# Unread products of constants in TensorE's waits, the overflow branch moved into the middle of the experts, and the wait of the up-projection split

## The chip, the core and the metric

The kernel runs on one core of one Trainium2 chip. A core has five engines that run their own instruction streams and meet at semaphores: TensorE (PE in the profile, its weight loads PEld), VectorE (DVE), ScalarE (ACT), GpSimd (POOL) and SyncE (SP), which issues the DMAs. The metric is the device time of one execution in microseconds, lower is better.

## The reference, cut to what matters

Two blocks of two layers each, over 256 tokens of width 1024, all in float32. What the change touches:

```python
def first_block(...):
    for l in range(DEPTH):                      # DEPTH = 2
        h = modulate(rms_norm(x, norm1_g[l]), sh1, sc1)
        x = x + g1[:, None, :] * token_mixer(h, ...)
        h = modulate(rms_norm(x, norm2_g[l]), sh2, sc2)
        x = x + g2[:, None, :] * hier_moe(h, ...)   # router, then 32 experts, top 2 of 8 in one of 4 groups

def hier_moe(...):
    ...
    sizes = jnp.bincount(flat_e, length=N_EXPERTS)  # any size is allowed
    hu = lax.ragged_dot(xs, w1, sizes)              # 1024 x 1024 for each expert
    ys = lax.ragged_dot(jax.nn.silu(h_gate) * h_up, w2, sizes)   # 512 x 1024

def second_block(...):
    for i in range(DEPTH):
        h = modulate_2(rms_norm_2(x, norm_g[i, 0]), sh1, sc1)
        y = attention_mixers(...) if i % 2 == 0 else fourier_mix(h) @ w_f
        x = x + g1 * rms_norm_2(y, norm_g[i, 1])
        h = modulate_2(rms_norm_2(x, norm_g[i, 2]), sh2, sc2)
        x = x + g2 * rms_norm_2(conv_ffn(h, ...), norm_g[i, 3])
```

## The kernel before

The tokens stay in SBUF, features on the partitions (`xT`, 8 tiles of 128x256). Each engine has a hand-written program (`pe_program`, `act_program`, ...); nothing is scheduled by a tool, so the order in the code is the order on the engine. An engine waits with `wait_ge` on counts that others raise.

**Banks.** PSUM banks `ps0` to `ps3` are handed out round robin by `bank.turn(name)`: who takes a turn waits until the bank's earlier holder is through, which `bank.until(name, counter, step)` has declared.

**A norm** (`NormMod`, with `Rstd`) runs over all engines: ACT squares the eight tiles of x (L729), PE sums them with 128x1 products (`pe_stats`, "stats" below), ACT takes the root (L777), DVE the reciprocal and two diagonal matrices (L782, L785), PE multiplies ones by the diagonal (`pe_spread`), DVE and ACT scale and shift, tile by tile, and for the split matmuls ACT and DVE make a high and a low part of each tile (L827, L860). Then the projection's products begin. **A post-norm** (`PostNorm`) comes after an output projection: ACT squares and sums the result in PSUM (L2621), ACT and DVE copy it out scaled (ACT L2633, DVE L2662), PE transposes it back (L2648) and DVE adds it to `xT` (L2665). In `postA` the result stands in all four of `ps0` to `ps3`; its own transposes go to other banks (`hbank`), and each bank of the four is free once its part is "copied". In `postF` the result stands in `ps4` to `ps7`.

**The router** ends in a chain of small operations on DVE (L1839 to L1883) that finds each token's two experts (`sel`) and their places, during which PE has only the counting products (128x32) to do. **The experts** go in 16 pairs. A pair `p` on PE: `pe_up` (32 matmuls, two row groups at a time), `pe_scatter(p - 1)`, `pe_gather(p + 1)`, a transposition (`pe_turn`), `pe_down` (16 matmuls). The weights, 12 MB a pair, come through 13 slots that SP refills in `sp_moe` as PE frees them. `pe_gather(p + 1)` needs one-hot places that DVE makes after it has worked off `pe_up(p)` (L2002, L2004, then L1952). A pair holds up to 64 tokens of an expert. Where an expert has more, a branch (`flag > 0`, code in `pe_over_all` and its like on ACT, DVE and SP) does the rest; with these inputs it is jumped over. It stands at the end of the 16 pairs, after the last scatter:

```python
pe_scatter(pe, l, m, NE // 2 - 1)
pe.wait_ge(*dve_moe["flag", l])
flag = pe.op.value_load(ints[0:1, l * 16 + 15:l * 16 + 16], min_val=0, max_val=8)
with pe.op.If(flag > 0):
    pe_over_all(pe.part(), l, m)
```

What follows in layer 0 is `norm1[1]`; in layer 1 it is `pe_heads`, whose first products work on the context and need no norm.

Of the kernel before, what the change touches and what calls it, by code (L numbers as in the profile page):

```python
# [18 lines left out]
NE = 32  # L19
# [205 lines left out]
def build(nc, A, out):  # L225
    CST_W = sum(w for _, w in CONST_COLS.values())
    with ExitStack() as ctx:
# [184 lines left out]
        def mm3(pe, out_, a, b, start, stop, **kw):  # L412
            mm(pe, out_, a[0], b[1], start, False, **kw)
            mm(pe, out_, a[1], b[0], False, False, **kw)
            return mm(pe, out_, a[0], b[0], False, stop, **kw)

        def sp_fm(sp, name, W, a0, by):

            load(sp, name, by_rows(W[:, a0:a0 + 256]), 8, 256)
            for m in range(2):  # L420
                unit((*name, m), name, 8, 256, lambda v, m=m: v[:, :, m * 128:(m + 1) * 128], by)
# [373 lines left out]
        class NormMod:  # L795
# [32 lines left out]

            def pe(self, pe, gap=0):
                self.r.pe_stats(pe)  # L830
                self.r.pe_spread(pe)
                pe_mods(pe, gap)

            def dve(self, dve, gap=0):
# [853 lines left out]
        def sp_moe(sp, l):  # L1688
# [6 lines left out]
            n_load = 0  # L1695
            for p in range(NE // 2):
                for which, W, parts in (("w1", W1, 4), ("w2", W2, 2)):
                    for n in range(parts):
                        for e in (2 * p, 2 * p + 1):
                            if n_load == all_.index(12):  # L1700
                                sp.wait_ge(*pe_unit["o", l, 3, 1])
                            load(sp, (which, l, e, n), by_rows(W[e, n * 256:(n + 1) * 256, :]), 2, 1024, all_)
                            n_load += 1
# [3 lines left out]
            else:  # L1707
                sp_kv(sp, 0)
            sp.wait_ge(*dve_moe["flag", l])
            flag = sp.op.value_load(ints[0:1, l * 16 + 15:l * 16 + 16], min_val=0, max_val=8)  # L1710
            with sp.op.If(flag > 0):
                part = sp.part()
                for j in range(NOV):
                    part.wait_ge(*dve_over[l]["ints"])
                    part.wait_ge(*(pe_over[l]["scatter", j - 1] if j else pe_moe["scatter", l, 15]))
                    e = part.op.value_load(ints[0:1, l * 16 + j:l * 16 + j + 1], min_val=0, max_val=31)
# [81 lines left out]
        def pe_router(pe, l, m):  # L1798
            pe_tokens(pe, l, m, 3)
            pe_stats(pe, l, m, 3)  # L1800
            if l == 1:
                pe_turn_tokens(pe, ("ctx",), "ctx", act_pro)
# [171 lines left out]
        def pe_up(pe, l, m, p):  # L1974
            x3 = v3(m.x["x", l, p], 8)
            for half in range(2):
                pe.wait_ge(*bank.turn("up", l, p, half))
            pe.wait_ge(*act_moe["xg", l, p])
            pe.wait_ge(*dve_moe["xg", l, p])
            for k in range(8):  # L1980
                for half in range(2):
                    for e in range(2):
# [87 lines left out]
        def pe_moe_all(pe, l, m):  # L2070
            pe_gather(pe, l, m, 0)
            for p in range(NE // 2):
                pe_up(pe, l, m, p)
                if p:
                    pe_scatter(pe, l, m, p - 1)
# [8 lines left out]
            pe_scatter(pe, l, m, NE // 2 - 1)  # L2084
            pe.wait_ge(*dve_moe["flag", l])
            flag = pe.op.value_load(ints[0:1, l * 16 + 15:l * 16 + 16], min_val=0, max_val=8)
            with pe.op.If(flag > 0):
                pe_over_all(pe.part(), l, m)

        def act_moe_all(act, l, m):  # L2090
            act_gather(act, l, m, 0)
            for p in range(NE // 2):
                act_up(act, l, m, p)
                if (l, p) == (0, NE // 2 - 1):
# [8 lines left out]
                if (l, p) == (1, 2):  # L2103
                    normC.act_apply(act)
            act.wait_ge(*dve_moe["flag", l])
            flag = act.op.value_load(ints[0:1, l * 16 + 15:l * 16 + 16], min_val=0, max_val=8)
            with act.op.If(flag > 0):
                act_over_all(act.part(), l, m)

        def dve_moe_all(dve, l, m):  # L2110
            dve_gather(dve, l, m, 0)
            for p in range(NE // 2):
                dve_up(dve, l, m, p)
                if p + 1 < NE // 2:
# [3 lines left out]
                if (l, p) == (1, 1):  # L2118
                    normC.dve(dve)
            dve.wait_ge(*dve_moe["flag", l])  # L2120
            flag = dve.op.value_load(ints[0:1, l * 16 + 15:l * 16 + 16], min_val=0, max_val=8)
            with dve.op.If(flag > 0):
                dve_over_all(dve.part(), l, m)
            g2 = mods[:, l * 48 + 40:l * 48 + 48]
# [9 lines left out]
        def dve_over_all(dve, l, m):  # L2134
            P3, G3, xv, gv, tv, hv, yv = over_bufs(m)
            D_ = dve_over[l]
            ind3, gt3, prod3, p13 = v3(m.ind, NOV), v3(m.gate, 2), v3(m.prod, 2), v3(m.p1, 2)
            dve.wait_ge(*pe_moe["scatter", l, NE // 2 - 1])
            for j in range(NOV):
# [63 lines left out]
        def pe_over_all(pe, l, m):  # L2203
            P3, G3, xv, gv, tv, hv, yv = over_bufs(m)
            x3, h3 = v3(xv[:, 0:512], 8), v3(hv[:, 0:256], 4)
            slot = [v3(slot_at[2 + n][0], 2) for n in range(6)]
            for j in range(NOV):
                pe.wait_ge(*dve_over[l]["P", j])
# [399 lines left out]
        class PostNorm:  # L2608
# [31 lines left out]

            def pe(self, pe):
                for k in range(8):
                    for j in range(2):
# [308 lines left out]
        def pe_program(pe):  # L2952
# [4 lines left out]
            for l in range(2):  # L2957
                if l == 1:
                    norm1[l].pe(pe, 3)
                pe_mixer(pe, l, mix[l], norm1[l])  # L2960
# [4 lines left out]
            for l in range(2):  # L2965
                if l == 1:
                    normA[1].pe(pe)
                    pe_fourier(pe, normA[1])
# [3 lines left out]
                postA[l].pe(pe)  # L2972
                normF[l].pe(pe)
                pe_ffn_all(pe, l, ffn)
# [146 lines left out]
```

## Time and profile before

| | |
|---|---|
| median of 3 runs | 2311.27 us (2306.36 to 2318.2) |
| the profiled execution | 2302.7 us, of which 2300.9 us from its first to its last instruction |
| PE busy | 2134.7 us, 93% |
| DVE, ACT, POOL busy | 42%, 30%, 12% |
| granted TensorE clock, mean | 0.972 of 2.4 GHz |

The granted clock has two levels, 1.00 (2.4 GHz) and 0.50 (1.2 GHz). A window's row that says 0.50 lay wholly at the lower one.

### The profile page before, as it was taken

The numbers are of one execution on the slowest core, as the hardware profiler recorded it, in microseconds if no ns is written. First come the engines' busy times: TensorE is split into PE (matmuls) and PEld (weight loads), VectorE is DVE, ScalarE is ACT, GpSimd is POOL, SyncE is SP. The second block draws the span as 40 slices with busy tenths as digits, with TensorE's granted clock in tenths as the row PEclk, the third lists the DMA queues.
The fourth block names the chain that finished last, engine by engine and source line by source line (L and its number), as shares of the span: only waits on it lengthen the run. The fifth ranks groups of instructions, "written<-read, shape, count | busy, mean of one in ns | idle before, by whom it ended". The sixth has DMA issues, their size and how long they took to land.

```text
span 2300.9 us, 30193 instructions
## 1 busy us (share of the span) xinstructions
PE 2134.7 (93%) x12867; PEld 1500.7 (65%) x12867; DVE 963.1 (42%) x1892; ACT 685.9 (30%) x1224; POOL 284.1 (12%) x145
## 2 busy tenths in 40 slices
PE   6999888999999989998899999999998899998998
PEld 4787674555544567777645555554774699978997
DVE  2466632212111136566312221221245577756776
ACT  3434421101101034353211110110203555555554
POOL 4554420000000034554000000000000000000000
PEclk8999989999999989999899999999999999998999
DMA  9965669999999976657689999999355375334651
GB/s 347 325 226 206 242 241 380 409 409 409 409 409 409 408 275 224 220 220 293 271 347 389 409 409 409 409 409 404 126 206 213 130 235 187 109 115 167 199 173 48
DMA packets 242742, 657.30 MB, mean 286 GB/s; under 512 B 12923, under 2 KB 116837, under 8 KB 230184
## 3 DMA queue, kind: packets, MB, share of 16 engines
q1 hardware_dynamic: 239936, 651.74, 74.8%
q8 instruction: 105, 1.72, 0.3%
q0 software_dynamic: 1184, 2.08, 0.3%
q10 hardware_dynamic: 1480, 1.45, 0.2%
q14 instruction: 37, 0.30, 0.0%
HBM read 654.17 MB, written 1.06 MB: 285 GB/s over the span
## 4 chain that ended last, share of the span: by engine, by line
PE 86%; DVE 10%; ACT 3%; issue 1%; DMA 0%; POOL 0%; ACTq 0%; DVEq 0%
PE ps L410 85%; DVE AR L1971 2%; DVE AR L747 1%; DVE AR L2018 1%; PE ps L2648 0%; DVE ARr L1646 0%; DVE AR L1231 0%; ACT AR L818 0%; ACT AR L2621 0%; ACT HBr L387 0%; PE ps L2472 0%; DMA hT<-in_onehot 0%; DVE ringr L393 0%; DVE AR L1114 0%; ACT hTr L827 0%
## 5 line engine op out<-in xcount | busy, mean ns | idle before, releaser
L410 PE MATMUL ps<-ring,AR 128*64 128x512 f32 (+2 forms) x2016 | 514.7, 577 | 31.4 <-DVE AR L2018 31.4
L410 PE MATMUL ps<-XLr,HBr 128*128 128x256 f32 x1280 | 375.5, 293 | 22.1 <-DVE ringr L393 6.9
L410 PE MATMUL ps<-AR 128*128 128x128 f32 (+6 forms) x2088 | 380.9, 345 | 14.0 <-DVE AR L1952 7.5
L410 PEld LDWEIGHTS ps<-ring,AR 128*64 128x64 f32 (+1 forms) x2016 | 196.8, 140 | 268.9 <-issue 264.0
L410 PEld LDWEIGHTS ps<-AR 128*128 128x128 f32 (+2 forms) x2088 | 290.0, 192 | 119.5 <-issue 76.4
L410 PE MATMUL ps<-hTr,ringr 128*128 128x256 f32 x1280 | 366.5, 286 | 0.0
L410 PE MATMUL ps<-hTr,HBr 128*128 128x256 f32 x1280 | 366.2, 286 | 0.0
L393 POOL TENSOR_TENSOR ringr<-ring,HBr 128x1024 fp32r<-128x1024 f32 x110 | 266.3, 2436 | 777.6 <-ACT HBr L387 777.4
L387 ACT ACTIVATE HBr<-ring 128x1024 fp32r<-128x1024 f32 x260 | 266.3, 1050 | 196.6 <-PE ps L410 179.9
L410 PEld LDWEIGHTS ps<-XLr,HBr 128*128 128x128 f32 x1280 | 249.4, 195 | 43.6 <-issue 24.8
L410 PEld LDWEIGHTS ps<-hTr,ringr 128*128 128x128 f32 x1280 | 250.2, 195 | 2.1 <-issue 1.0
L410 PEld LDWEIGHTS ps<-hTr,HBr 128*128 128x128 f32 x1280 | 249.8, 195 | 0.0
L393 DVE TENSOR_TENSOR ringr<-ring,HBr 128x1024 fp32r<-128x1024 f32 x150 | 179.5, 1223 | 82.0 <-ACT HBr L387 81.7
L2002 DVE SCALAR_TENSOR_TENSOR AR<-AR,ps 128x512 f32<-128x512 f32 x32 | 22.0, 688 | 438.1 <-ACT AR L1997 438.1
L410 PE MATMUL ps<-HB,AR 128*64 128x512 f32 x464 | 154.7, 597 | 8.0 <-DVE AR L2018 8.0
L1997 ACT ACTIVATE AR<-ps 128x512 f32<-128x512 f32 x32 | 19.1, 598 | 418.8 <-PE ps L410 418.8
L410 PE MATMUL ps<-HBr,ARr 128*128 128x512 f32 x416 | 135.9, 395 | 0.0
L2047 DVE COPY AR<-ps 128x512 f32<-128x512 f32 x32 | 22.1, 692 | 237.8 <-PE ps L410 237.8
L410 PE MATMUL ps<-XL,AR 128*64 128x512 f32 x240 | 108.1, 593 | 6.1 <-DVE AR L2018 3.2
L410 PE MATMUL ps<-hT,AR 128*64 128x512 f32 x240 | 108.1, 593 | 3.2 <-DVE AR L2018 3.2
L410 PE MATMUL ps<-ring,crep 128*32 128x512 f32 x704 | 97.2, 632 | 13.5 <-DVE mods L709 12.9
L2042 ACT ACTIVATE AR<-ps 128x512 f32<-128x512 f32 x32 | 19.1, 597 | 282.9 <-PE ps L410 282.9
(311 smaller groups left out, 2593.9 us busy)
## 6 DMA issues: line engine op xcount, KB each, us to landing
ring<-in_w_expert_in SPq DMA_DIRECT2D x155, 1024.0 KB, 14.8
ring<-in_w_expert_out SPq DMA_DIRECT2D x81, 1024.0 KB, 11.0
ring<-in_mod_w SPq DMA_DIRECT2D x48, 1024.0 KB, 6.6
ring<-in_ffn_w_up SPq DMA_DIRECT2D x44, 1024.0 KB, 5.2
ring<-in_w_in SPq DMA_DIRECT2D x40, 1024.0 KB, 5.6
ring<-in_w_ada SPq DMA_DIRECT2D x40, 1024.0 KB, 8.2
HB<-in_w_expert_in SPq DMA_DIRECT2D x35, 1024.0 KB, 14.6
HB<-in_w_expert_out SPq DMA_DIRECT2D x23, 1024.0 KB, 12.3
```

Of the source, the lines that this page charges most:

```text
L387: act.op.activation(hi, raw, ACT.Copy).then_inc(*act_hi.inc(*name))
L393: lane.op.tensor_tensor(lo, sel(chunk(of, k, w)), hi.bitcast(F32), ALU.subtract).then_inc(*count.inc(*name))
L410: return pe.op.matmul(out_, lhsT, rhs, start=start, stop=stop, **kw)
L747: dve.op.reciprocal(rs[:, 0:n], rs[:, 0:n]).then_inc(*dve_norm.inc(tag, "rstd"))
L1971: dve.op.tensor_scalar(m.x["x", l, p][:, k * 128:(k + 1) * 128], bank["xg", l, p, 1][:, c], m.coef[:, k:k + 1], m.shift[:, k:k + 1], ALU.m ...
L1997: act.op.activation(m.th["th", l, p], bank["up", l, p, 0][:, :], ACT.Tanh, scale=0.5).then_inc(*act_moe.inc("th", l, p))
L2002: dve.op.scalar_tensor_tensor(t, t, 1.0, bank["up", l, p, 0][:, :], ALU.add, ALU.mult).then_inc(*dve_moe.inc("gated", l, p))
L2018: dve.op.tensor_copy(m.h["h", l, p], bank["turn", l, p][:, :]).then_inc(*dve_moe.inc("turn", l, p))
L2042: act.op.activation(m.y["y", l, p][:, 0:512], bank["down", l, p, 0][:, :], ACT.Copy).then_inc(*act_moe.inc("y", l, p))
L2047: dve.op.tensor_copy(m.y["y", l, p][:, 512:1024], bank["down", l, p, 1][:, :]).then_inc(*dve_moe.inc("y", l, p))
```

## The change

Four things, all on the order and the waits; the values that reach the output are those of before.

1. `pe_busy(pe, n, name)` issues `n` products of constants (ones by 512 columns of the constant table, full array, float32) into a bank that nobody reads. It is called: 5 and 3 times in the routers of layers 0 and 1 (between the stats and the counting products), 2 before the stats of `norm1[1]` and 1 between its stats and its spread, 1 and 2 likewise around the spread of `normA[1]`, 1 and 3 around that of both `normF`, 3 at the head of each of the four post-norms. In all 34 products.
2. The overflow branch goes from the end of the 16 pairs to the head of pair 9, on all four engines; `pe_scatter(8)` moves ahead of it.
3. SP takes its branch before it loads pair 9, not after all loads.
4. `pe_up` waits for ACT's half of the gathered tokens before the first four k, and for DVE's half only before k = 4.

```diff
+        def pe_busy(pe, n, *name):
+            pe.wait_ge(*q_cst0["all"])
+            pe.wait_ge(*bank.turn("busy", *name))
+            for _ in range(n):
+                t = mm(pe, bank[("busy", *name)][:, :], C("ones"), cst[:, 0:512], True, True)
+            t.then_inc(*pe_pro.inc("busy", *name))
+            bank.until(("busy", *name), pe_pro, "busy", *name)
...
-            def pe(self, pe, gap=0):
+            def pe(self, pe, gap=0, busy=0):
                 self.r.pe_stats(pe)
+                if busy:
+                    pe_busy(pe, 1, self.tag, "diagonal")
                 self.r.pe_spread(pe)
                 pe_mods(pe, gap)
+                if busy > 1:
+                    pe_busy(pe, busy, self.tag, "applied")
...
             for p in range(NE // 2):
+                if p == OVER_AT:
+                    sp_over(sp, l, W1, W2)
...
             pe_stats(pe, l, m, 3)
+            pe_busy(pe, 5 - 2 * l, "router", l)
...
-            pe.wait_ge(*act_moe["xg", l, p])
-            pe.wait_ge(*dve_moe["xg", l, p])
             for k in range(8):
+                pe.wait_ge(*(act_moe if k < 4 else dve_moe)["xg", l, p])
...
         def pe_moe_all(pe, l, m):
             pe_gather(pe, l, m, 0)
             for p in range(NE // 2):
+                if p == OVER_AT:                       # OVER_AT = 9
+                    pe_scatter(pe, l, m, p - 1)
+                    pe.wait_ge(*dve_moe["flag", l])
+                    flag = pe.op.value_load(ints[0:1, l * 16 + 15:l * 16 + 16], min_val=0, max_val=8)
+                    with pe.op.If(flag > 0):
+                        pe_over_all(pe.part(), l, m)
                 pe_up(pe, l, m, p)
-                if p:
+                if p and p != OVER_AT:
                     pe_scatter(pe, l, m, p - 1)
...
             pe_scatter(pe, l, m, NE // 2 - 1)
-            pe.wait_ge(*dve_moe["flag", l])
-            flag = pe.op.value_load(ints[0:1, l * 16 + 15:l * 16 + 16], min_val=0, max_val=8)
-            with pe.op.If(flag > 0):
-                pe_over_all(pe.part(), l, m)
...
             def pe(self, pe):
+                pe_busy(pe, 3, self.tag)
                 for k in range(8):
...
                 if l == 1:
-                    norm1[l].pe(pe, 3)
+                    pe_busy(pe, 2, "norm1", l)
+                    norm1[l].pe(pe, 3, 1)
...
-                    normA[1].pe(pe)
+                    normA[1].pe(pe, 0, 2)
...
-                normF[l].pe(pe)
+                normF[l].pe(pe, 0, 3)
```

PE in layer 0, from the last products of `pe_down(8)` to the head of pair 9, before the change (`64x512` are expert products, `128x256` the scatter, `128x128` with AR alone the gather):

```order
L410 MATMUL ps<-ring,AR 64x512
L410 MATMUL ps<-HB,AR 64x512
L410 MATMUL ps<-AR 128x256 [waits dve_moe,act_moe]
L410 MATMUL ps<-AR 128x256 x7
L410 MATMUL ps<-AR 128x128 [waits dve_moe]
L410 MATMUL ps<-AR 128x128 x15
```

There the last products of `pe_up(9)` are followed by `pe_scatter(8)`, and that by `pe_gather(10)`. With the change the scatter stands at the head of pair 9, behind `pe_down(8)`, and the branch behind it (`128x64` is the first row of the part that is jumped over):

```order
L410 MATMUL ps<-ring,AR 64x512
L410 MATMUL ps<-AR 128x256 [waits dve_moe,act_moe]
L410 MATMUL ps<-AR 128x256 x7
L2096 TENSOR_LOAD ints
L2096 ISA x2
L2097 COMPARE_AND_BRANCH
L410 MATMUL ps<-AR 128x64 [waits dve_over0]
```

and after `pe_up(9)` the gather follows at once:

```order
L410 MATMUL ps<-ring,AR 64x512
L410 MATMUL ps<-HB,AR 64x512
L410 MATMUL ps<-AR 128x128 [waits dve_moe]
L410 MATMUL ps<-AR 128x128 x15
L1950 MATMUL ps<-cst,AR 128x128 [waits dve_moe]
L1950 MATMUL ps<-cst,AR 128x128
```

So the scatter, with its wait for both halves of pair 8's result, now stands between pair 8's down-projection and pair 9's up-projection, and no longer between `pe_up(9)` and `pe_gather(10)`.

PE at the head of `postA[0]` before the change (L675 turns a row of modulation, L2648 are the post-norm's transposes):

```order
L675 MATMUL ps<-cst,modrow 128x128 [waits dve_mod]
L675 MATMUL ps<-cst,modrow 128x128 x3
L2648 MATMUL ps<-cst,AR 128x128 [waits dve_norm,act_norm]
L2648 MATMUL ps<-cst,AR 128x128
L2648 MATMUL ps<-cst,AR 128x128 [waits dve_att]
```

The transposes follow the modulation row as soon as the scaled copies are there. With the change (L684 and L2676 are the same two lines):

```order
L684 MATMUL ps<-cst,modrow 128x128 [waits dve_mod]
L684 MATMUL ps<-cst,modrow 128x128 x3
L410 MATMUL ps<-cst 128x512 [waits act_norm]
L410 MATMUL ps<-cst 128x512 x2
L2676 MATMUL ps<-cst,AR 128x128 [waits dve_norm]
L2676 MATMUL ps<-cst,AR 128x128
```

The three unread products stand ahead of the transposes and wait for a count of ACT (`act_norm`): their turn falls on the bank that ACT's first scaled copy frees.

Behind the last scatter of either layer PE now goes on at once: in layer 0 with two unread products and the stats of `norm1[1]`, in layer 1 with `pe_heads`.

## Rows read from the trace of the kernel before

**Rows 1.** The page: busy time, share of the span, instructions

```profile
PE 2134.7 (93%) x12867; PEld 1500.7 (65%) x12867; DVE 963.1 (42%) x1892; ACT 685.9 (30%) x1224; POOL 284.1 (12%) x145
```

**Rows 2.** Windows: us, busy time (instructions) of each engine, then granted clock, DMA share, GB/s

```profile
825.00:838.00 13.00, 10.38 (x46) 8.00 (x50) 3.51 (x13) 6.68 (x13) 3.15 (x2) 0.50 0.16 50
...
320.00:333.00 13.00, 6.65 (x31) 6.43 (x31) 9.48 (x49) 3.15 (x9) 0.00 (x0) 0.50 0.63 254
```

**Rows 3.** Waits of PE, 345 to 808 us: us in total, times, longest

```profile
PE ps L410 <- DVE AR L2018: 24.1, 15, 1.6
```

**Rows 4.** Timeline of PE, layer 0's router: start, us, what, idle before

```profile
325.88 2.34 PE L410 MATMUL ps<-AR,cst 128*128 128x32 f32 x10 [5.64 <-DVE AR L1871]
328.93 5.97 PE L410 MATMUL ps<-AR 128*128 128x128 f32 x32 [0.71 <-DVE AR L1952]
...
336.56 0.61 PE L410 MATMUL ps<-XL,AR 128*64 128x512 f32 x1 [1.45 <-DVE AR L1971]
```

**Rows 5.** Timeline of PE, layer 1's router

```profile
1117.26 6.04 PE L410 MATMUL ps<-AR 128*128 128x128 f32 x32 [0.71 <-DVE AR L1952]
...
1124.99 0.61 PE L410 MATMUL ps<-XL,AR 128*64 128x512 f32 x1 [1.48 <-DVE AR L1971]
```

**Rows 6.** Timeline of PE, scatter and gather of a later pair; gather of pair 1

```profile
412.33 7.29 PE L410 MATMUL ps<-AR 128*128 128x256 f32 x48
...
353.55 5.46 PE L410 MATMUL ps<-AR 128*128 128x128 f32 x32 [3.03 <-DVE AR L1952]
```

**Rows 7.** The line of PE's branch: ns min/median/max, first and last start

```profile
L2087 PEldq COMPARE_BRANCH  x2: 6219/6272/6326, 820.2 to 1616.9; - x2
```

**Rows 8.** Timeline of PE, end of layer 0's experts and norm1[1]

```profile
819.22 3.69 PE L410 MATMUL ps<-AR 128*128 128x256 f32 x16 [0.91 <-DVE AR L2047]
826.54 6.99 PE L410 MATMUL ps<-cst,AR 128*128 128x1 f32 x32 [3.63 <-ACT AR L729]
834.60 1.22 PE L410 MATMUL ps<-diag,cst 128*128 128x256 f32 x2 [1.07 <-DVE diag L785]
```

**Rows 9.** The chain that ended last, 815 to 842 us: start, us, what

```profile
823.47 2.77 ACT AR L729 x7
```

**Rows 10.** Timeline of PE, end of layer 1's experts

```profile
1623.29 8.83 PE L410 MATMUL ps<-AR,ring 128*128 128x256 f32 x32 [3.44 <-ACT AR L729]
```

**Rows 11.** Timeline of ACT and of PE, postA[0] and normF[0]

```profile
1824.72 1.84 ACT L2633 ACTIVATE AR<-ps,smal 128x512 f32<-128x512 f32 x3 [0.23 <-DVE smal L2660]
...
1825.62 2.99 PE L2648 MATMUL ps<-cst,AR 128*128 128x128 f32 x16 [2.18 <-DVE AR L2662]
1828.45 3.70 PE L410 MATMUL ps<-cst,AR 128*128 128x1 f32 x32
...
1837.00 0.55 PE L410 MATMUL ps<-XLr,HBr 128*128 128x256 f32 x1 [2.55 <-DVE XLr L860]
```

**Rows 12.** Timeline of PE, normF[1], normA[1], and 128x512 products at either clock

```profile
2086.13 6.82 PE L410 MATMUL ps<-cst,AR 128*128 128x1 f32 x32
...
2030.56 2.60 PE L2648 MATMUL ps<-cst,AR 128*128 128x128 f32 x16 [2.38 <-DVE AR L2662]
...
2041.04 9.23 PE L410 MATMUL ps<-ring,hT 128*128 128x258 f32 x28 [1.79 <-ACT hT L818]
...
1734.04 2.84 PE L410 MATMUL ps<-AR 128*128 128x512 f32 x6 [2.11 <-DVE AR L2372]
1741.80 1.92 PE L410 MATMUL ps<-AR 128*128 128x512 f32 x2
```

**Rows 13.** Timelines of SP, pair 9's loads, and of ACT, ends of pair 8's down- and pair 9's up-projection

```profile
580.89 11.67 SPq L342 DMA_DIRECT2D ring<-in_w_expert_in  x7
...
610.83 0.60 ACT L2042 ACTIVATE AR<-ps 128x512 f32<-128x512 f32 x1 [8.75 <-PE ps L410]
624.57 0.60 ACT L1997 ACTIVATE AR<-ps 128x512 f32<-128x512 f32 x1 [13.14 <-PE ps L410]
```

**Rows 14.** The page: issues of DMA, KB each, median us to landing

```profile
ring<-in_w_expert_in SPq DMA_DIRECT2D x155, 1024.0 KB, 14.8
```

More of the change, by code:

```diff
@@ L1708, in sp_moe, with sp_over @@
                 sp_kv(sp, 0)
+        OVER_AT = 9
+        def sp_over(sp, l, W1, W2):
             sp.wait_ge(*dve_moe["flag", l])
@@ L1714, in sp_moe @@
                     part.wait_ge(*dve_over[l]["ints"])
-                    part.wait_ge(*(pe_over[l]["scatter", j - 1] if j else pe_moe["scatter", l, 15]))
+                    part.wait_ge(*(pe_over[l]["scatter", j - 1] if j else pe_moe["scatter", l, OVER_AT - 1]))
                     e = part.op.value_load(ints[0:1, l * 16 + j:l * 16 + j + 1], min_val=0, max_val=31)
@@ L2092, in act_moe_all @@
             for p in range(NE // 2):
+                if p == OVER_AT:
+                    act.wait_ge(*dve_moe["flag", l])
+                    flag = act.op.value_load(ints[0:1, l * 16 + 15:l * 16 + 16], min_val=0, max_val=8)
+                    with act.op.If(flag > 0):
+                        act_over_all(act.part(), l, m)
                 act_up(act, l, m, p)
@@ L2104, in act_moe_all @@
                     normC.act_apply(act)
[L2105 to L2108, printed above, removed]
         def dve_moe_all(dve, l, m):
@@ L2112, in dve_moe_all @@
             for p in range(NE // 2):
+                if p == OVER_AT:
+                    dve.wait_ge(*dve_moe["flag", l])
+                    flag = dve.op.value_load(ints[0:1, l * 16 + 15:l * 16 + 16], min_val=0, max_val=8)
+                    with dve.op.If(flag > 0):
+                        dve_over_all(dve.part(), l, m)
                 dve_up(dve, l, m, p)
@@ L2119, in dve_moe_all @@
                     normC.dve(dve)
[L2120 to L2123, printed above, removed]
             g2 = mods[:, l * 48 + 40:l * 48 + 48]
@@ L2137, in dve_over_all @@
             ind3, gt3, prod3, p13 = v3(m.ind, NOV), v3(m.gate, 2), v3(m.prod, 2), v3(m.p1, 2)
-            dve.wait_ge(*pe_moe["scatter", l, NE // 2 - 1])
+            dve.wait_ge(*pe_moe["scatter", l, OVER_AT - 1])
             for j in range(NOV):
@@ L2206, in pe_over_all @@
             slot = [v3(slot_at[2 + n][0], 2) for n in range(6)]
+            pe.wait_ge(*act_moe["GT", l, OVER_AT])
+            pe.wait_ge(*dve_moe["xg", l, OVER_AT])
             for j in range(NOV):
```

## The prediction, made before the run

> **What bounds the kernel now.** I read the page first: TensorE is busy for 93% of the span [rows 1]. What is taken from or laid onto PE's own stream counts in full, nearly everywhere. That goes for the experts too, though their DMA is full: from 345 to 808 us PE never waited for a weight. Its only waits are 15 for DVE's copy of the turned tile, 24.1 us in all [rows 3], and one of 3.0 us at pair 0 [rows 6]. A load lands 14.8 us after its issue in the median [rows 14]; pair 9's first loads are issued from 580.9 us, and pair 8's down-projection, which pair 9 follows, ends at 610.8 us [rows 13]. So the weights are there about 610.8 - 580.9 - 14.8 = 15 us early. The experts are bound by PE, and idle time that is put into them comes out at the end.
>
> Next the granted clock: it is 0.50 in stretches that follow idle time or stretches with nothing but narrow products, in the routers, in the norms, and behind the branch [rows 2]. What half clock costs is read from twins. The 32 records of a norm's stats took 6.99 us at half and 3.70 us at full clock [rows 8, 11]. The gather's 32 records took 5.97 and 6.04 us behind the routers [rows 4, 5]; in a later pair, gather and scatter together took 7.29 us and the scatter alone takes 3.69 us, so the gather at full clock takes 3.6 us [rows 6, 8]. A float32 product of 512 columns is two records, and six took 2.84 us at full clock, two 1.92 us at half [rows 12]. Of each some 0.25 us is the last record's way through the array, paid once in a row; so an unread product costs 0.86 us at full and 1.7 us at half clock.
>
> **The change, part by part.**
>
> Router of layer 0: -4.2 us. PE is idle for 5.64 us until 325.88 [rows 4], so from 320.2 us. Five unread products take 4.3 us at full and 8.6 us at half clock. The clock was 0.50 from 320 us on [rows 2]; with the first two at half and the rest at full they take 6.0 us and end 0.1 us late. At full clock the gather is 2.4 us shorter and the counting products and what follows some 0.5 us. The split wait takes off the 1.45 us for which PE waited for DVE's half [rows 4]. Together -4.2. Bounds: all five at half make it 2.9 us late, with only the split won, +1.4; all at full, -4.4.
>
> Router of layer 1: -3.8 us. 6.04 becomes 3.6, and 1.48 us of wait goes [rows 5]. Bounds -1.4 (clock not kept) and -3.9.
>
> The middle of the experts, each layer: +9.4 us. Here every step stands on PE's stream. (a) The scatter of pair 8 must wait for pair 8's results: 0.91 us, as the last scatter does now [rows 8]; before, pair 9's up-projection covered that. (b) The branch: it takes 6.2 to 6.3 us on PE's sequencer, both times, from shortly after the scatter begins [rows 7]. In layer 0 PE's next product came 3.63 us after the scatter, in layer 1 3.44 us [rows 8, 10]; I take 3.6. (c) Between the up-projection of pair 9 and the gather of pair 10 there is no scatter any more, and the gather needs places that DVE makes after the up-projection. The only pair without a scatter there today is pair 0, and there PE waits 3.03 us [rows 6]. (a) to (c) are 7.5 us. (d) Idle times of 3.6 and of 3.0 us were each followed by half clock (the windows behind 825 us, and a gather of 5.46 us) [rows 2, 8, 6], which cost 5.46 - 3.6 = 1.9 us; of two such in a layer I count one. Two layers make +18.8 us; bounds +15 (clock kept) and +22.6. What waits behind the branch on DVE and ACT is pair 9's gating, which starts 624.57 - 610.83 = 13.7 us after pair 8's down-projection [rows 13]; SP's loads have the 15 us above.
>
> The price of (b) is where the skill and the trace differ. By the Trainium skill, "Advanced Engine Details and Errata", Control Flow Timing, a compare-and-branch takes some 108 ns; with that the middle would cost 7 us less and the sum below would be -5 us. "Runtime: NRT & Kernel Launch", Instruction fetch mechanics, says that a taken branch to a target outside the fetched pages forces a fetch and stalls the engine, and that speaks against this change; the 6.2 us in the trace agree with it. I keep the trace's.
>
> End of layer 0's experts and norm1[1]: -5.2 us. The scatter ends at 819.22 + 3.69 = 822.9. ACT's first square begins at 823.5 [rows 9], but PE's stats only at 826.54, and then at half clock, to 833.5 [rows 8]. Now: two unread products to 824.6, stats at full clock, 3.7 us, to 828.3. The rest of the chain (root, diagonal, spread 1.07 us behind the stats) moves with it; the one product ahead of the spread fits into that 1.07 us at full clock. Bounds: -1.9 (stats at half clock) and -5.5.
>
> End of layer 1's experts: -5.3 us. The context's products wait for nothing but the branch: 3.44 us go. And the 32 records behind it took 8.83 us [rows 10], in part at half clock; a record of 512 columns takes 0.86 / 2 = 0.43 us at full clock, one of 256 columns 0.215, and 32 of them 6.9: 1.9 us come back. Bounds -3.4 and -5.3.
>
> The two post-norms postA with normF: +3.0 us. The three products at the head of postA get the bank of ACT's first scaled copy, so they start no sooner than 1824.72 + 0.6 = 1825.3 us, 0.3 us before the transposes did [rows 11]. They take 2.6 us and push the transposes by 2.3 us, and with them the additions, the squares, the stats: 4.6 us for the two. At normF one product before the spread fits into 1.07 us at full clock and costs 0.65 us at half; the three behind it take 2.6 us of a wait of 2.55 us [rows 11], and 5.1 at half: I add 1 us for each. Gained: the stats of normF[1], 6.82 us today [rows 12], take 3.7, and its spread 0.5 us less. 4.6 + 2.0 - 3.6 = 3.0. Bounds 0 and +8.
>
> postF[0] and normA[1]: -1.5 us. Three products take 2.6 us in a gap of 2.38 us, +0.2; the first 28 Fourier records took 9.23 us [rows 12], for some 6 us of it at half clock, of which up to 2.9 us can come back; the two products ahead of them may run at half clock themselves (+1). postF[1], at the very end: +0.2, and as much back in the transposes: 0.
>
> Sum: -4.2 - 3.8 + 18.8 - 5.2 - 5.3 + 3.0 - 1.5 = +1.8 us on the profiled 2302.7 us, so 2304.5. That execution lies 8.6 us below the median of the three (2311.27), so the forecast is 2313 us. A measurement of this kernel tells changes of about 0.5% (11.6 us) from none; this is 0.1%.
>
> **The rivals.**
>
> *The middle is covered (faster), 0.14.* If in other executions the weights come later than in this trace, PE would wait for them in late pairs, and what the branch costs in the middle would be given back there. For it: DMA is full, and the cover shrinks from pair to pair. Against it: not one wait for a load [rows 3], and 15 us of cover at pair 9. It would give 1.8 - 18.8 = -17 us, 2294 us.
>
> *The branch in the middle is dearer (slower), 0.09.* It falls where the DMA queues are fullest. If the fetch of its target stands behind the weights as a load does, 14.8 us instead of the few in which it came at the end, each layer loses some 10 us more: +22 us, 2333. It decides from 5 us a branch. Against: at the end of layer 1 the DMA was busy too, and the branch took as long as in layer 0 [rows 7].
>
> *The unread products don't hold the clock (slower), 0.08.* Then the change doesn't do what it says: the gathers (2 x 2.4), the stats (3.3 and 3.1) and the Fourier products (1.5) stay as they are, and the fillers at half clock push what is behind them, 2.6 us more in each postA: 1.8 + 4.8 + 6.4 + 1.5 + 5.2 = +20 us, 2331. For it: transposes and 128x1 products between them are narrow; against: dense 512-column products ran at full clock wherever they stood for long.
>
> *The forecast, within 0.5%, 0.69.* Its terms of both signs are each of some 20 us, so an error of a third in either moves the result by 6 or 7 us, still inside.
>
> **The numbers.** Of the 0.69, 0.01 goes to either side beyond the bound, for terms that err together. Faster 0.14 + 0.01 = 0.15, slower 0.09 + 0.08 + 0.01 = 0.18, same 0.67. Range: from 2296, just above the covered middle, to 2328, short of the two slower rivals, which leaves out about 0.2; the likeliest case alone spans 2304 to 2322.
>
> **What would show it.** In the profile of the changed kernel: the gather behind either router in 3.6 us, and pair 0's up-projection right behind the transposed gates; at pair 9 of either layer, an idle time of PE of 0.9 us before the scatter, one of 3.5 us behind it and one of 3.0 us before the next gather, and pairs of the same length before and behind it; stats of 3.7 us in norm1[1]; PE on the context's products within 0.1 us of the last scatter; in postA the transposes 2.3 us later against ACT's copies. Wrong it would be if PE's wait at pair 9 were followed by shorter pairs (the middle is covered), if the branch took more than 11 us, or if the granted clock were 0.50 behind the fillers.

## The result, and the profile after

The changed kernel takes 2321.87 us in the median of 22 runs (2307.45 to 2327.78), the kernel before 2312.39 us (22 runs). The ratio is 1.0038, with a 95% interval of 1.0026 to 1.0049: slower by 0.4%, inside the 0.5% that the forecast called "same", and its time is inside the forecast's range. The interval leaves out the forecast's own +0.1%, though: the change cost 9.5 us by the medians and not 1.8. The forecast's time, 2313 us, was 8.9 us too low; 1.1 of these are the kernel before, whose median went from 2311.27 to 2312.39 us with more runs. Time and granted clock go together over the 22 runs: 2307.45 us had 0.983, 2327.78 us had 0.971. The profiled execution (2312.39 us at 0.978) is 9.5 us faster than its median, and that of the kernel before 9.7 us (2302.7 against 2312.39), so the two traces can be set side by side.

The middle of the experts first. The waits of PE from 345 to 820 us, in total, times and longest, in the changed kernel:

```profile
PE ps L410 <- DVE AR L2038: 24.9, 16, 1.6
PE ps L410 <- DVE AR L1973: 6.1, 2, 3.1
PE ps L410 <- issue: 3.6, 1, 3.6
PE ps L410 <- DVE AR L2067: 0.9, 1, 0.9
```

Against [rows 3] three waits are new: 3.6 us that no other engine explains ("issue"), a second one of 3.1 us for the gather's places (before there was only that of pair 0, [rows 6]), and 0.9 us for pair 8's result. The timeline of PE at pair 9 of layer 0 shows where they lie, and the line of the branch what it takes:

```profile
610.73 3.69 PE L410 MATMUL ps<-AR 128*128 128x256 f32 x16 [0.88 <-DVE AR L2067]
617.99 10.94 PE L410 MATMUL ps<-ring,AR 128*64 128x512 f32 x49 [3.56 <-issue]
635.00 3.84 PE L410 MATMUL ps<-AR 128*128 128x128 f32 x32 [3.06 <-DVE AR L1973]
```

```profile
L2097 PEldq COMPARE_BRANCH  x2: 6079/6154/6229, 611.7 to 1409.2; - x2
```

Scatter after 0.88 us, the up-projection 3.56 us behind the scatter, the gather 3.06 us behind the up-projection: 7.5 us. In layer 1 the three are 0.88, 3.23 and 3.07 us. No load was late: the waits name no DMA.

The routers: the first fence is layer 0, the second layer 1 (start, us, what, idle before).

```profile
323.38 5.98 PE L410 MATMUL ps<-cst 128*128 128x512 f32 x10
329.20 1.26 PE L410 MATMUL ps<-AR,cst 128*128 128x32 f32 x10
331.59 3.84 PE L410 MATMUL ps<-AR 128*128 128x128 f32 x32 [1.12 <-DVE AR L1973]
```

```profile
1109.72 2.82 PE L410 MATMUL ps<-cst 128*128 128x512 f32 x6
1112.38 1.91 PE L573 MATMUL ps<-cst,ring 128*128 128x128 f32 x16
1115.60 1.27 PE L410 MATMUL ps<-AR,cst 128*128 128x32 f32 x10 [1.31 <-DVE AR L1895]
1117.99 5.46 PE L410 MATMUL ps<-AR 128*128 128x128 f32 x32 [1.12 <-DVE AR L1908]
```

In layer 0 the five unread products fill the wait and the gather runs at full clock (3.84 us where [rows 4] have 5.97). In layer 1 the gather still takes 5.46 us: a half-clock stretch came all the same. The wait for DVE's half is gone in both.

The ends of the experts and `norm1[1]`, in layer 0 and then layer 1:

```profile
826.35 3.69 PE L410 MATMUL ps<-AR 128*128 128x256 f32 x16 [0.91 <-DVE AR L2067]
829.88 1.88 PE L410 MATMUL ps<-cst 128*128 128x512 f32 x4
831.60 3.82 PE L410 MATMUL ps<-cst,AR 128*128 128x1 f32 x32
```

```profile
1625.24 3.69 PE L410 MATMUL ps<-AR 128*128 128x256 f32 x16 [0.91 <-DVE AR L2067]
1628.77 7.07 PE L410 MATMUL ps<-AR,ring 128*128 128x256 f32 x32
```

The stats take 3.82 us where [rows 8] have 6.99, and the context's products start with no gap and take 7.07 us where [rows 10] have 8.83 behind a gap of 3.44.

`postA[0]`: three unread products, the transposes, the stats of `normF[0]`.

```profile
1833.94 4.49 PE L410 MATMUL ps<-cst 128*128 128x512 f32 x6 [2.03 <-ACT AR L2660]
1838.23 3.06 PE L2676 MATMUL ps<-cst,AR 128*128 128x128 f32 x16
1841.12 3.63 PE L410 MATMUL ps<-cst,AR 128*128 128x1 f32 x32
```

They wait for ACT's first scaled copy, as forecast. They took 4.3 us until the transposes began, partly at half clock, and push these by 4.1 us against the kernel before, where the forecast had 2.3; in `postA[1]` the push is 2.5 us.

### The profile page after: what moved, and what is told of

The parts are those of the page before. It is cut to its first block, busy times and chain, and to the rows that moved or that the text cites. A ratio compares the mean times of both kernels' runs of the same rounds, so it can differ in the third digit from the quotient of the medians.

```text
span 2310.6 us, 30329 instructions
## 1 busy us (share of the span) xinstructions
PE 2156.5 (93%) x12935; PEld 1494.2 (65%) x12935; DVE 962.5 (42%) x1892; ACT 685.4 (30%) x1224; POOL 284.1 (12%) x145
## 4 chain that ended last, share of the span: by engine, by line
PE 85%; DVE 9%; ACT 2%; DMA 1%; issue 1%; POOL 1%; SPq 0%; DVEq 0%; ACTq 0%; POOLq 0%
PE ps L410 84%; DVE AR L1992 2%; DMA ring<-in_w_in 1%; DVE AR L756 1%; DVE AR L2038 1%; ACT AR L827 0%; DVE ARr L1659 0%; DVE AR L1244 0%; PE ps L2499 0%; PE ps L2676 0%; ACT hTr L836 0%; POOL cols L516 0%; DVE AR L1973 0%; DVE AR L1127 0%; ACT HBr L387 0%
## 5 line engine op out<-in xcount | busy, mean ns | idle before, releaser
L410 PE MATMUL ps<-AR 128*128 128x128 f32 (+6 forms) x2088 | 381.1, 345 | 22.8 <-DVE AR L1973 13.4
L410 PE MATMUL ps<-XLr,HBr 128*128 128x256 f32 x1280 | 373.2, 292 | 21.8 <-DVE ringr L393 6.9
```

Source lines behind the costliest of these rows:

```text
L410: return pe.op.matmul(out_, lhsT, rhs, start=start, stop=stop, **kw)
```

## The experiments

Ratios are against runs of the kernel before on the same chip, with 95% intervals. Every diff is against the changed kernel.

**e1_branch_alone.** Only the branch moved; no unread products, and the wait of the up-projection not split:

```diff
-            pe_busy(pe, 5 - 2 * l, "router", l)
...
-                pe.wait_ge(*(act_moe if k < 4 else dve_moe)["xg", l, p])
+            pe.wait_ge(*act_moe["xg", l, p])
+            pe.wait_ge(*dve_moe["xg", l, p])
...
-                pe_busy(pe, 3, self.tag)
...
-                    pe_busy(pe, 2, "norm1", l)
-                    norm1[l].pe(pe, 3, 1)
+                    norm1[l].pe(pe, 3)
...
-                    normA[1].pe(pe, 0, 2)
+                    normA[1].pe(pe)
...
-                normF[l].pe(pe, 0, 3)
+                normF[l].pe(pe)
```

> The kernel before with nothing but the branch moved to pair 9: no unread products, the wait of the up-projection not split. Theory (every step at pair 9 stands on PE's stream, as the changed kernel's profile shows: 0.9 for the scatter's wait, 3.6 for the branch, 3.1 for the next gather): +7.6 us in each layer, plus some 1 us where the clock falls; given back at the end of layer 1's experts 3.4 to 5.3 us, and at the end of layer 0's, where the squares of the norm still bind, 2 to 3 us. Sum 15.2 + 1 - 5.3 - 2.5 = +8.4 us against the kernel before, ratio 1.0036 (1.002 to 1.006). Rival (pairs behind the branch get shorter, the middle is covered): -7 us, ratio 0.997.

Measured: 2324.09 us, ratio 1.0061 (1.0048 to 1.0074). The move alone makes the kernel slower, by 14 us where 8.4 were expected, just above the expected 1.006; the covered middle is out. At the end of layer 0 its trace won 5.6 us where 2 to 3 were expected: with no unread product in front, the stats of `norm1[1]` took 3.81 us, as in the changed kernel:

```profile
835.96 3.81 PE L410 MATMUL ps<-cst,AR 128*128 128x1 f32 x32 [1.02 <-ACT AR L738]
```

**e2_branch_back.** The branch back at the end on all engines:

```diff
-                if p == OVER_AT:
-                    pe_scatter(pe, l, m, p - 1)
-                    pe.wait_ge(*dve_moe["flag", l])
-                    ...
-                if p and p != OVER_AT:
+                if p:
...
             pe_scatter(pe, l, m, NE // 2 - 1)
+            pe.wait_ge(*dve_moe["flag", l])
+            ...
```

> The changed kernel with the branch back at the end of the experts on all engines; unread products and split wait stay. Theory: routers -3.5 and -2.6 us, norm1[1] -1 us (its stats at full clock, but two products in front of them), postA[0] +4.3 and postA[1] +2.2, the Fourier products -2.7, the stats of normF[1] -2.9, the others 0: -6 us against the kernel before, ratio 0.9974 (0.995 to 0.999). Rival (the loss of the change is not in the branch but in the unread products): 1.002 or above.

Measured: 2305.59 us, ratio 0.9992 (0.9978 to 1.0006). The unread products are not the loss, but bring less than expected: -2 us by the ratio (-5 to +1.4), not -6. In its trace the two products ahead of `norm1[1]` stand behind the branch's idle time, the stats behind them still take 6.83 us, and over the end of the layer and the norm (815 to 842 us) PE lost 2.6 us against the kernel before:

```profile
822.30 2.75 PE L410 MATMUL ps<-cst 128*128 128x512 f32 x4 [3.88 <-issue]
824.85 6.83 PE L410 MATMUL ps<-cst,AR 128*128 128x1 f32 x32
```

**e3_no_postA.** No unread products at the head of the two `postA`:

```diff
-                pe_busy(pe, 3, self.tag)
+                if self.tag[0] != "pA":
+                    pe_busy(pe, 3, self.tag)
```

> The changed kernel without the three unread products at the head of the two postA; those of postF and all others stay. Theory (they get a bank that ACT's first scaled copy frees, and push the transposes by 2.2 us at full and 4.3 us at half clock): transposes right behind the scaled copies again, 6.5 us less than the changed kernel's profile, so +3 us against the kernel before, ratio 1.0013 (1.000 to 1.003). Rival (they hold the clock for the stats behind them and pay for themselves): as the changed kernel, 1.0038, with stats of 6.9 us in normF.

Measured: 2311.72 us, ratio 1.0015 (0.9999 to 1.0031). The size is the expected one, the reason is not. In its trace the transposes start right behind the copies, but the stats of `normF[0]` now take 6.83 us, so the expected 4.3 us are not in this trace:

```profile
1833.55 3.41 PE L2677 MATMUL ps<-cst,AR 128*128 128x128 f32 x16 [2.19 <-DVE AR L2691]
1836.75 6.83 PE L410 MATMUL ps<-cst,AR 128*128 128x1 f32 x32
```

**e4_short_jump.** Overflow code for one block; beyond it overflow is left out:

```diff
-NOV = 7
+NOV = 1
```

> The changed kernel with the overflow code for one block of 64 tokens instead of seven (NOV = 1), so that the branch jumps over about a seventh of the instructions; overflow beyond one block is left out, and with these inputs nothing is jumped into. Theory A (any taken branch out of what has been fetched costs a fetch of its target, however far): the branch still takes 6.1 to 6.3 us on PE, PE idle 3.6 us behind the scatter, ratio 1.0038 as the changed kernel. Theory B (the price grows with what is jumped over, or a near target is already there): below 2.5 us, PE idle under 1 us there, 5 to 7 us less in all, ratio 1.001.

Measured: 2306.1 us, ratio 0.9973 (0.9957 to 0.9989), 0.65% or 15 us less than the changed kernel. The line of the branch, and PE at pair 9:

```profile
L2097 PEldq COMPARE_BRANCH  x2: 358/369/380, 608.6 to 1403.2; - x2
```

```profile
607.63 3.69 PE L410 MATMUL ps<-AR 128*128 128x256 f32 x16 [0.88 <-DVE AR L2067]
611.25 10.94 PE L410 MATMUL ps<-ring,AR 128*64 128x512 f32 x49
628.27 3.84 PE L410 MATMUL ps<-AR 128*128 128x128 f32 x32 [3.06 <-DVE AR L1973]
```

0.37 us instead of 6.15, and no idle time behind the scatter; the waits of 0.88 and 3.06 us stay. So the branch itself is cheap, and the 6.2 us belong to the length of what it jumps over. Theory A fell; theory B had the mechanism, but expected 5 to 7 us less, not 15.

**e7_jump_of_3.** The same with `NOV = 3`, executed once.

> The changed kernel with overflow code for three blocks of 64 (NOV = 3; the rest of the overflow is left out): what the branch on PE takes. If the price is one step (target already fetched, or not): 0.36 or 6.2 us. If it grows with the length: 2 to 3 us.

```profile
L2097 PEldq COMPARE_BRANCH  x2: 6019/6112/6206, 613.8 to 1419.1; - x2
```

6.1 us, as over seven blocks: the price is a step between one block and three, and doesn't grow from there to seven. By the Trainium skill, "Runtime: NRT & Kernel Launch", Instruction fetch mechanics, a taken branch stalls when its target lies outside what has been fetched; the three lengths agree (0.37, 6.11, 6.15 us). This kernel is also a second trace of the changed one, since what runs is the same; its execution took 2325.19 us at clock 0.970, 3.3 us above that median. PE at pair 9:

```profile
612.90 3.69 PE L410 MATMUL ps<-AR 128*128 128x256 f32 x16 [0.88 <-DVE AR L2067]
620.10 13.75 PE L410 MATMUL ps<-ring,AR 128*64 128x512 f32 x49 [3.50 <-issue]
639.93 5.22 PE L410 MATMUL ps<-AR 128*128 128x128 f32 x32 [3.07 <-DVE AR L1973]
```

The waits are those of the changed kernel to 0.1 us, but the 49 expert records take 13.75 us instead of 10.94, and the gather 5.22 instead of 3.84. The windows of this kernel show the granted clock (0.50, third figure from the end) behind either wait, in both layers:

```profile
618.97:625.70 6.73, 5.61 (x14) 1.71 (x16) 0.00 (x0) 0.00 (x0) 0.00 (x0) 0.50 0.84 335
639.50:642.80 3.30, 2.87 (x13) 2.88 (x14) 1.26 (x6) 0.00 (x0) 0.00 (x0) 0.50 1.03 412
1424.60:1431.30 6.70, 6.08 (x16) 1.77 (x18) 0.00 (x0) 0.00 (x0) 0.00 (x0) 0.50 0.70 278
1445.00:1448.30 3.30, 3.04 (x14) 3.04 (x15) 1.09 (x5) 0.00 (x0) 0.00 (x0) 0.50 1.01 405
```

**e5_hops.** All seven blocks, each in an If of its own on PE:

```diff
-                    with pe.op.If(flag > 0):
-                        pe_over_all(pe.part(), l, m)
+                    for j in range(NOV):
+                        with pe.op.If(flag > 0):
+                            pe_over_all(pe.part(), l, m, (j,))
```

> The changed kernel with its overflow code complete, but on PE each of the seven blocks stands in an If of its own, so that PE takes seven short jumps at pair 9 and no long one. Theory A (a jump as short as the one over a single block costs 0.36 us, whoever stands ahead of it): 7 x 0.36 = 2.5 us on the sequencer, most of it under the 2.7 us of scatter records that are still queued; PE idle under 1 us behind the scatter, ratio 0.998. Theory B (a taken jump drops what was fetched ahead, so that the second and later ones stall): 2 to 6 us each, PE idle for 10 us or more, ratio 1.01 or above.

Measured: 2342.67 us, ratio 1.0132 (1.011 to 1.0154). In layer 0 the first hop took 0.36 us and the six behind it 5.89, 5.78, 2.96, 0.22, 3.29 and 3.13; PE stood 19.27 us:

```profile
634.07 8.42 PE L410 MATMUL ps<-ring,AR 128*64 128x512 f32 x30 [19.27 <-issue]
```

So theory B holds: a jump over one block was cheap for the first and the fifth of the seven only, and layer 1 has the same pattern. Why the fifth was cheap isn't shown.

**e6_short_end.** `NOV = 1` (the rest of the overflow left out), branch at the end as in e2_branch_back, no unread products in `postA` as in e3_no_postA.

> Branch back at the end of the experts, overflow code for one block of 64 only (the rest of the overflow is left out), no unread products at the head of the two postA; all other unread products and the split wait stay. Theory (the branch's price is the length of the jump; what the changed kernel lost in the middle beyond it is the scatter's and the gather's wait, 4.0 us a layer): PE idle under 1 us behind either last scatter, norm1[1]'s stats at full clock from about 2 us behind the scatter, no wait of 3.1 us for DVE's places but that of pair 0: 2305.6 of the kernel with the branch back, less 6.5 in postA, less 4 and 5.3 at the two ends = 2290 us, ratio 0.991 (0.989 to 0.994). Rival (a shorter jump only moves the idle time to the next wait): 0.996.

Measured: 2299.09 us, ratio 0.994 (0.9918 to 0.9962). In layer 0 the end has no idle time behind the scatter, as expected, and of the waits of 3.1 us only that of pair 0 is left. In layer 1 the context's products begin at once, but after six of their records PE stands for 2.22 us that no other engine explains:

```profile
1614.77 5.77 PE L410 MATMUL ps<-AR,ring 128*128 128x256 f32 x26 [2.22 <-issue]
```

So there the idle time did partly move on, as the rival had it. The size is 0.3% short of the expected 0.991, and the interval holds the rival's 0.996 too.

**e8_routers_alone.** The kernel before with the routers' unread products and the split wait: the diffs of e1 for the post-norms and norms, and that of e2.

> The kernel before with the unread products of the two routers and the split wait, nothing else. Theory: router of layer 0 -3.5 us (gather at full clock, split wait), router of layer 1 -3 us (the turning of the context is pushed by 2 us, but it and the gather run at full clock), so -6.5 us, ratio 0.9972 (0.996 to 0.999). Rival (the clock falls later instead, at the next narrow stretch): within 2 us of before, 1.000.

Measured: 2308.9 us, ratio 0.9983 (0.997 to 0.9997). A gain of 0.7 to 7 us: the theory's 6.5 is inside, at its end, no change at all is just outside, and so the rival, within 2 us, isn't excluded. Its trace shows what the rival said: each router's stretch is 2.6 us shorter, but 1.3 us of it in layer 0 and 1.1 in layer 1 are gone again by the next pairs, where PE's idle time is that of before and its products take longer. In layer 0 it is the gather of pair 1, 5.46 us in [rows 6]:

```profile
353.96 6.69 PE L410 MATMUL ps<-AR 128*128 128x128 f32 x32 [3.06 <-DVE AR L1972]
```

**e9_pair0.** PE's branch in pair 0, between the up-projection and the gather (overflow would not be computed); no products in `postA`:

```diff
-                if p == OVER_AT:
-                    pe_scatter(pe, l, m, p - 1)
-                    pe.wait_ge(*dve_moe["flag", l])
-                    ...
                 pe_up(pe, l, m, p)
-                if p and p != OVER_AT:
+                if p == 0:
+                    pe.wait_ge(*dve_moe["flag", l])
+                    ...
+                if p:
                     pe_scatter(pe, l, m, p - 1)
```

> All unread products but those of the two postA, the split wait, all seven blocks of overflow code; PE's branch stands in pair 0 between the up-projection and the gather of pair 1, the other engines' at pair 9, and the scatter of pair 8 is back behind pair 9's up-projection. What is left out: with overflow this kernel would not compute it, since its code may not run there; with these inputs it is jumped over. Theory (the branch costs what of its 6.2 us is neither under queued products nor under a wait that is there anyway): at pair 0 PE's queue holds some 2.6 us and the wait for DVE's places is 3.1 us, so the idle time grows from 3.1 to about 3.7 us, and nothing else stalls for it: as the kernel with the short jump at the end plus 1.2 us, 2300 us, ratio 0.995 (0.992 to 0.997). Rival (stalls add up whatever the place): idle time 6 us or more at pair 0, ratio 0.998 or above.

Measured: 2289.43 us, ratio 0.9925 (0.9903 to 0.9947), the lowest of all, though its interval overlaps that of e6_short_end. The branch took what it always takes over seven blocks, and the wait for the gather's places did not grow:

```profile
L2097 PEldq COMPARE_BRANCH  x2: 6169/6170/6171, 343.3 to 1123.7; - x2
```

```profile
349.98 2.38 PE L410 MATMUL ps<-AR 128*128 128x128 f32 x15 [3.06 <-DVE AR L1973]
```

343.32 + 6.17 = 349.5 us, and the gather starts at 349.98: the whole stall lies under products that were already queued (until 349.98 - 3.06 = 346.9) and under a wait that was there anyway.

**e10_end_no_postA.** The diffs of e2 and e3 together; complete in function.

> Complete in function: the kernel before plus the unread products but those at the head of the two postA, plus the split wait; the branch is where it was. Theory: the kernel with the branch back (2305.6) less the 6.5 us of postA seen in traces: 2300 us, ratio 0.9955 (0.994 to 0.998). Rival (the clock that those products held pays for them): 0.999.

Measured: 2309.51 us, ratio 1.0003 (0.9993 to 1.0013). The theory fell: taking the products out of `postA` brought nothing here; if anything, e2_branch_back with them is better. Its trace has the stats at half clock again:

```profile
1828.76 6.83 PE L410 MATMUL ps<-cst,AR 128*128 128x1 f32 x32
```

**e11_also_no_norm1.** The kernel e10_end_no_postA without the three products around `norm1[1]`:

```diff
-                    pe_busy(pe, 2, "norm1", l)
-                    norm1[l].pe(pe, 3, 1)
+                    norm1[l].pe(pe, 3)
```

> As the kernel before it in this series, also without the three unread products around norm1[1], which with the branch at the end cost 2.2 us there while the stats still ran at half clock. Theory: stats 1.7 to 2.2 us earlier, so 2 us less than its twin, ratio 0.9945. Rival (they do shorten the half-clock stretch in most executions): no gain or 2 us more.

Measured: 2302.32 us, ratio 0.9982 (0.9969 to 0.9996): 0.2% or 5 us better than its twin (the intervals overlap by 0.0003), where the two traces differ by 3.3 us at this place.

**e12_bridge.** As e11, with two unread products ahead of the branch in each layer:

```diff
             pe_scatter(pe, l, m, NE // 2 - 1)
+            pe_busy(pe, 2, "end", l)
             pe.wait_ge(*dve_moe["flag", l])
```

> As its twin without norm1's unread products, but two unread products stand between the last scatter and the branch in each layer. Theory (they lie under the branch's 6.4 us and shorten PE's idle time): idle time 3.7 -> about 2.9 us, the branch 0.9 us later, and what follows (stats of norm1[1] 7.0, 32 context records 8.8) at full clock where idle time was what let it fall: 3.7 and 6.9. Sum 0.9 + 0.9 - 3.3 - 1.9 = -3.4 us against the twin, ratio 0.993. Rival (2.9 us of idle time let the clock fall as 3.7 did): 1.8 us more than the twin.

Measured: 2300.68 us, ratio 0.9968 (0.9944 to 0.9993). Against e11 (0.9982) the intervals overlap, so a gain over the twin is not shown; the expected 0.993 is outside. The trace is of its slowest execution; PE's idle time behind the four records fell to 2.52 us, and the stats took 5.26, between the two clocks:

```profile
819.02 1.88 PE L410 MATMUL ps<-cst 128*128 128x512 f32 x4
823.41 5.26 PE L410 MATMUL ps<-cst,AR 128*128 128x1 f32 x32 [2.52 <-ACT AR L738]
```

e11 and e12 are complete in function and faster than both kernels, by 0.2 and 0.3% against the kernel before; e12 has the lowest median of the complete ones.

## Why the prediction was right, point by point

The ratio fell into the class where it was put, and nearly all mechanisms were the named ones, but the change cost 9.5 us where 1.8 were forecast. Terms were mis-sized, and one was left out: what the clock does in stretches that the change doesn't touch. The table gives what each stretch added to PE's lateness: the start of the same instruction in the later trace minus its start in the kernel before, end of the stretch less its beginning (times of the kernel before). The last column does it for e7_jump_of_3.

| stretch, us | forecast | changed kernel | e7_jump_of_3 |
|---|---|---|---|
| router of layer 0, 315 to 337 | -4.2 | -4.2 | -2.6 |
| middle of layer 0, 600 to 645 | +9.4 | +8.0 | +12.2 |
| end of layer 0, norm1[1], 815 to 842 | -5.2 | -5.2 | -4.9 |
| router of layer 1, 1100 to 1130 | -3.8 | -2.6 | -1.9 |
| middle of layer 1, 1400 to 1440 | +9.4 | +9.3 | +12.1 |
| end of layer 1, 1612 to 1640 | -5.3 | -3.7 | -3.7 |
| postA and normF, both layers | +3.0 | +4.0 | +4.0 |
| postF[0], normA[1], 2028 to 2050 | -1.5 | -2.3 | -2.3 |
| postF[1], at the very end | 0 | -0.7 | -0.7 |
| all else, where nothing was changed | 0 | +6.8 | +10.0 |
| sum | +1.8 | +9.4 | +22.2 |

"All else" is clock. Of the changed kernel's 6.8 us, 3.2 stood before the first changed instruction, so the change didn't cause them; 1.1 came between 1130 and 1400 and 3.1 between 1640 and 1815 us, and 0.7 went between 842 and 1100. In all of these but the first 57 us, PE's idle time is that of before to 0.1 us; only its products take longer. (In the first 57 us PE stood 2.7 us longer, yet came out less than 0.5 us later.) The trace of e7 is of a slow execution, 3.3 us above its median, and that of the kernel before of a fast one, 9.7 us below: so of its +22.2 us some 13 are such a draw.

**The middle.** (a) 0.88, (b) 3.56, (c) 3.06: forecast 0.9, 3.6, 3.0. Shown by the waits, and by e4, which took away (b) and left the others. What is uncertain is (d), the clock: "of two such in a layer I count one", 1.9 us. In the changed kernel's own trace the middle cost 8.0 and 9.3 us, in that of e7 12.2 and 12.1, outside the bound of 11.3, because the clock fell behind both waits in both layers. The traces of e1 and e3, with the same middle, have 11.0 and 9.1, 7.9 and 10.7. The mean of the eight is 10.0 us against the forecast 9.4: the count was fair, the bounds were too narrow, and the middle is not where most of the 7.7 us were missed. e4 took away two idle times, 6.8 us together, and won 15 us by the medians. What is over that can only be clock or noise, since nothing else was changed, but not clock in the middle alone: its trace ends 13.4 us earlier than the changed kernel's, 7.9 of them won at pair 9.

**The price of the branch.** Right to take the trace's 6.2 us; e4 and e7 show that the price hangs on how much is jumped over. With one block instead of seven the changed kernel is faster than the kernel before, at 0.9973 (e4, which leaves the rest of the overflow out).

**Routers.** The first one as forecast in the profiled execution. In layer 1 the turning of the context, which I had not put behind the unread products, moved by 2.4 us, and the gather stayed at half clock: -2.6 where the term was -3.8. e8 gave both routers 0.7 to 7 us, where the forecast had 8.0: a term mis-sized by at least 1 us, and in the trace of e7, with -4.5 for both, by 3.5. The forecast also stopped counting too early. In eleven of the twelve traces with the routers' products, 1.1 to 2.9 us were lost between 1130 and 1400 us, where e1 without them lost none. Net of that, layer 1's router gave 1.5 us in the changed kernel's trace.

**Ends.** End of layer 0 and the start of layer 1's context products came as forecast; but towards 1640 us a stretch of half clock that the kernel before didn't have took 1.7 us back, and at 1700 us (times of the kernel before) another one as much again, in the traces of the changed kernel, e7, e1 and e3. The first row is a window of the kernel before, the second one of the changed kernel that is 5 us later, as it is there; the granted clock is the third figure from the end:

```profile
1700.00:1703.00 3.00, 3.00 (x15) 2.63 (x14) 2.86 (x5) 0.00 (x0) 0.00 (x0) 1.00 0.89 366
1705.00:1708.00 3.00, 3.00 (x8) 2.12 (x7) 2.93 (x6) 0.00 (x0) 0.00 (x0) 0.55 0.93 339
```

So the term of -5.3 us was worth -2.0 in the end, the largest single miss that both traces share (the second 1.7 us stands under "all else"); why the clock fell there isn't shown. That the products ahead of `norm1[1]` help isn't shown at all. The forecast laid the stats at full clock to them, but e1 has the branch moved and no such products, and its stats took 3.81 us and the stretch from 815 to 842 us gave 5.6 us, against 3.82 and 5.2 with them. What brought the clock back there is then most likely that the branch's idle time was gone. Behind the branch the products cost time (e10 against e11).

**postA and normF.** The sum nearly held (+3.0 and +4.0), the reasoning did not. I read the stats of `normF[0]`, 3.70 us in [rows 11], as what the kernel always does; in six of the nine executions traced without postA's products they took 6.83. So the products pay back about what they push. e3 against the changed kernel gained 0.2%, e10 against e2 lost 0.1%: whether they help stays open. Around `normA[1]` (2028 to 2050 us) the products did more than forecast: 2.2 to 2.3 us less in eight of the eleven traces with them, 0.8 us more in e1 and e8 without them.

**Rivals.** The covered middle: excluded by e1 (1.0061) and by the waits. The dearer branch in the middle: 6.08 and 6.23 us, no dearer than at the end. Products that don't hold the clock: half of it happened. In the changed kernel's trace layer 0's gather and the stats of `norm1[1]` and `normF[0]` behind them ran at full clock (3.84, 3.82 and 3.63 us), though the stats of `norm1[1]` did so in e1 without them; layer 1's gather did not (5.46), nor did the stats behind the branch in e2 (6.83); so they gave less than forecast, but not nothing.

What was luck: the forecast set +21.8 against -20.0 us, and what it missed, 7.7 us, happened to be less than the 0.5% that separates "same" from the rest. It did not foresee that the change would be slower beyond the noise.

## What to carry to other kernels

A branch that is never taken into its body can cost 6 us on TensorE if the body is long. Put it where queued products and a wait that exists anyway cover it (e9: no cost seen in the trace, in a kernel that as it stands would not compute the overflow), or keep the body short (e4: 0.37 us); don't chain short jumps (e5: 21.6 us). Before a piece of work is moved between two stages, ask which waits it covered where it was: here the scatter had hidden 3.1 us of DVE's work and its own 0.9.

Here unread products were worth their time in the routers' waits, if not by much (e8), and around `normA[1]`; behind the branch's idle time they only pushed (e2, e10), and at `norm1[1]` taking the idle time away did their work (e1). Count what they bring some tens of us further on as well, since part of it was lost again there (e8). Where the clock moves, one trace is one draw: read a duration from several executions before it becomes a term.

## What was not expected of the hardware

- The price of a jump is a step: 0.37 us over one block, 6.11 over three, 6.15 over seven. Seven short jumps in a row took 21.6 us in layer 0 (0.36 for the first, 0.22 to 5.89 for the others).
- The stall runs beside queued products: in e9 PE's products went on for 3.6 us after the branch began (343.3 to 346.9 us).
- Of the same waits of 3.5 and 3.1 us, half clock followed neither in layer 0 of the changed kernel's trace, only the first in its layer 1, and both in that of e7. What decides it can't be read from these traces.
